# First MLP: ten inner tiles of the second half by seven block products, and the state space set-up within the first half

## The reference

```python
def _sq_relu_mlp(h, w_up, w_down):
    u = jax.nn.relu(h @ w_up)          # w_up: 1024 x 4096
    return (u * u) @ w_down            # w_down: 4096 x 1024

for i in range(DEPTH):                 # DEPTH = 2
    hn = _rmsnorm(h, norm_attn[i])
    h = h + _even_mixer(...) if i % 2 == 0 else h + _odd_mixer(...)
    h = h + _sq_relu_mlp(_rmsnorm(h, norm_mlp[i]), w_up[i], w_down[i])
```

## Time and profile before

| | |
|---|---|
| time, median of 3 runs | 2095.04 us (2094.91 to 2095.3) |
| profiled execution: its time | 2094.85 us |
| profiled execution: its span | 2092.7 us |
| instructions in the span | 35077 |
| busy share: TensorE matmul, weight load, VectorE, ScalarE, GpSimd | 99%, 87%, 65%, 42%, 40% |

### The profile page before, as it was taken

The page is one execution under the profiler, slowest core; times in us unless marked ns, Lnnn a source line. Parts: engine busy times, 40 slices in busy tenths (PEclk is TensorE's granted clock), DMA queues, the critical chain, the costliest instruction groups (busy, mean ns, idle before and its releaser), DMA issues.

```text
span 2092.7 us, 35077 instructions
## 1 busy us (share of the span) xinstructions
PE 2079.1 (99%) x14278; PEld 1826.3 (87%) x14278; DVE 1355.1 (65%) x2083; ACT 879.5 (42%) x1454; POOL 829.0 (40%) x388
## 2 busy tenths in 40 slices
PE   9999999999999999999999999999999999999998
PEld 9998899999999777798898788888888788988897
DVE  6678766625723395675855769576774577666865
ACT  5368644223323493443434423344433433433344
POOL 3343434434444453423234443333434443344332
PEclk9999999999999999999999999999999999999999
DMA  6620245233433602323343465233333332433341
GB/s 180 168 59 2 57 136 150 88 117 105 136 91 102 180 2 81 101 87 106 85 117 97 131 136 159 71 84 89 88 91 91 91 94 79 122 91 100 89 122 61
DMA packets 375695, 211.18 MB, mean 101 GB/s; under 512 B 26915, under 2 KB 368132, under 8 KB 374648
## 3 DMA queue, kind: packets, MB, share of 16 engines
q1 hardware_dynamic: 365230, 192.62, 32.6%
q10 hardware_dynamic: 10314, 16.41, 2.8%
HBM read 196.97 MB, written 15.40 MB: 101 GB/s over the span
## 4 chain that ended last, share of the span: by engine, by line
PE 65%; issue 22%; POOL 10%; DVE 2%; ACT 0%; DMA 0%; POOLq 0%; SPq 0%; DVEq 0%; ACTq 0%
PE acc L1268 15%; PE acc L1269 15%; PE acc L1270 14%; POOL w_lo L1038 9%; PE acc L1358 2%; PE ops L1427 2%; PE acc L1679 1%; PE acc L1671 1%; PE acc L1669 1%; PE tps L1367 1%; PE acc L1141 1%; PE ops L1421 1%; PE acc L1142 1%; PE acc L1143 1%; PE tps L1679 1%
## 5 line engine op out<-in xcount | busy, mean ns | idle before, releaser
L1038 POOL TENSOR_TENSOR w_lo<-raw,w_hi 128x1024 fp32r<-128x1024 f32 x278 | 688.2, 2476 | 964.8 <-ACT w_hi L1999 954.3
L1999 ACT ACTIVATE w_hi<-raw 128x1024 fp32r<-128x1024 f32 x277 | 293.4, 1059 | 839.9 <-PE acc L1270 810.5
L1268 PE MATMUL acc<-hr_hi,w_hi 128*128 128x512 f32 x1056 | 421.5, 399 | 0.3 <-POOL w_lo L1038 0.3
L1270 PE MATMUL acc<-hr_hi,w_lo 128*128 128x512 f32 x1056 | 417.7, 396 | 0.0
L1269 PE MATMUL acc<-hr_lo,w_hi 128*128 128x512 f32 x1056 | 417.6, 395 | 0.0
L1268 PE MATMUL acc<-hn_hi,w_hi 128*128 128x264 f32 (+1 forms) x840 | 246.8, 294 | 0.4 <-POOL w_lo L1038 0.4
L1270 PE MATMUL acc<-hn_hi,w_lo 128*128 128x264 f32 (+1 forms) x840 | 244.2, 291 | 0.0
L1269 PE MATMUL acc<-hn_lo,w_hi 128*128 128x264 f32 (+1 forms) x840 | 244.2, 291 | 0.0
L1268 PEld LDWEIGHTS acc<-hr_hi,w_hi 128*128 128x128 f32 x1056 | 198.5, 188 | 48.6 <-issue 1.5
L1270 PEld LDWEIGHTS acc<-hr_hi,w_lo 128*128 128x128 f32 x1056 | 198.4, 188 | 47.9
L1269 PEld LDWEIGHTS acc<-hr_lo,w_hi 128*128 128x128 f32 x1056 | 198.5, 188 | 47.1 <-issue 0.7
(11 more groups left out here) (551 smaller groups left out, 4389.0 us busy)
## 6 DMA issues: line engine op xcount, KB each, us to landing
raw<-in_w_up SPq DMA_DIRECT2D x64, 512.0 KB, 4.4
raw<-in_w_in SPq DMA_DIRECT2D x56, 512.0 KB, 3.8
raw<-in_w_down SPq DMA_DIRECT2D x40, 512.0 KB, 3.6
blocks<-in_w_down SPq DMA_DIRECT2D x32, 384.0 KB, 3.4
raw<-in_w_ffn_gate SPq DMA_DIRECT2D x22, 512.0 KB, 3.9
raw<-in_w_ffn_up SPq DMA_DIRECT2D x22, 512.0 KB, 3.8
raw<-in_w_in_even SPq DMA_DIRECT2D x18, 512.0 KB, 6.9
blocks<-in_w_ffn_down SPq DMA_DIRECT2D x16, 384.0 KB, 3.5
```

The source lines that it names most:

```text
L1038: nc.gpsimd.tensor_tensor(w_lo[:, part], raw[:, slot], w_hi[:, part].bitcast(F32), ALU.subtract).then_inc(sems["lo"], T.up("lo"))
L1268: mm(out, w_hi[:, part, w0 + k, :], xh, start=s0, stop=False)
L1270: ins = mm(out, w_lo[:, part, w0 + k, :], xh, start=False, stop=s1)
L1999: fn(w_hi[:, n % 2], raw[:, n % 4], ACT.Copy).then_inc(sems["hi"], T.up("hi"))
```

## The change

The second half of the first MLP is split. Its first ten inner tiles (`first_part`) are made in pairs and their down projection is done by the 7 block products, with token halves of 264 columns; the six that are left (`left_up`, `left_down`) are done plainly, with one unit of 6 tiles for each output tile. The forms, sums and blocks get buffers of their own, some of which lie over the buffers of the set-up, so the set-up must be over before them: VectorE does two steps in tiles 11, 12 and 13 of `up00`, `kernel_products` stands after tile 1 of `down00` instead of tile 4, the turns of the tables follow after tiles 2 to 5, and tiles 5, 6 and 7 of `down00` take 4, 5 and 6 steps. `store_ca` stands at tile 1 of `first_part`. SyncE waits for the stored tables and for the first pair's sums before it loads the blocks. The helpers of the products take the part's number and pick buffers and widths by it. GpSimd's list is cut at the same places.

```diff
-PART_SIZES = (PART_TILES, PART_TILES, 10, PART_TILES)
+FIRST_TILES = 10
+PART_SIZES = (FIRST_TILES, PART_TILES, PART_TILES, 10, PART_TILES)
...
+    first_part = Projection("first_part", [[(w_up[0], MLP_HALF * P, 0, 8, "hn")]], FIRST_TILES, 2, peel=FIRST_TILES // 2)
+    left_up = Projection("left_up", [[(w_up[0], LEFT_AT * P, 0, 8, "hn")]], LEFT_TILES, 2, peel=LEFT_TILES // 2)
+    left_down = Projection("left_down", [[(w_down[0], 0, LEFT_AT, LEFT_TILES, "mid")]], DT, 4, peel=2)
...
-    for half in range(2):
-        order += [mlp_up(0, half), mlp_down(0, half)]
+    order += [mlp_up(0, 0), mlp_down(0, 0), first_part, left_up, left_down]
...
+            first_hi = sb(s, "first_hi", [P, 7, FIRST_TILES // 2, HALF], F32R)
+            first_lo = sb(s, "first_lo", [P, 7, FIRST_TILES // 2, HALF], F32R)
...
+            pair_first = sb(s, "pair_first", [P, 2, LEN])
+            sums_first = sb(s, "sums_first", [P, 4, HALF])
+            blocks_first = sb(s, "blocks_first", [P, 6, FIRST_TILES // 2, P])
...
+        def first_bank(q, ring):
+            b = q.g % 2 if q.part else (ring + q.g) % 2
+            return acc[b][:, 1, halves_of(q.part)[0]]
...
+            units(first_part)
+            for name in ("ends_out0", "ends_out1"):
+                T.saw(name, 4 * 16)
+                sp.wait_ge(sems[name], T.at(name))
+            sp.wait_ge(sems["ssm_out"], 4 * 16)
+            sp.wait_ge(sems["pair_sums"], 1)
+            part_blocks(0)
+            units(left_up)
+            units(left_down)
...
-                tables = {4: kernel_products, 5: lambda: (turn_powers(0), turn_kernel()),
-                          6: lambda: turn_powers(1), 7: lambda: turn_powers(2)}
...
-                project(by_name["up01"], None, None, None, {0: lambda: turn_powers(3)})
-                project(by_name["down01"], None, ("hidden_lo", MLP_HALF))
...
+                tables = {1: kernel_products, 2: lambda: (turn_powers(0), turn_kernel()),
+                          3: lambda: turn_powers(1), 4: lambda: turn_powers(2), 5: lambda: turn_powers(3)}
...
+                project(first_part)
+                down_by_products(0)
+                pe.wait_ge(sems["product_kept"], QUADS[2].done(P7))
+                project(left_up, None, None, lambda: pe.wait_ge(sems["product_kept"], QUADS[3].done(P7)))
+                project(left_down, None, ("hidden_lo", LEFT_TILES))
...
-                if m == 13:
+                if m == 1:
                     T.saw("ssm_tab", 3)
...
+                def hidden(m, s, t, b):
+                    inner(m, s, b)
+                    for _ in range(2 if m in (11, 12, 13) else 1):
+                        next(setup)
+                    inner_low(m, s)
+
+                def plain(m, s, t, b):
+                    dve.wait_ge(sems[f"full{b}"], T.at(f"full{b}"))
+                    store(v.tensor_tensor(h[:, m, :], h[:, m, :], acc1[b], ALU.add), b)
+                    for _ in range({5: 4, 6: 5, 7: 6}.get(m, 1)):
+                        next(setup)
...
+                project(by_name["up00"], hidden)
+                project(by_name["down00"], plain)
+                assert not list(setup)
...
+                inner_part(0, first_part, pair_first, acc1, rstd[:])
+                project(left_up, hidden_left)
+                residual(left_down, 8, False)
```

More of the change, by code:

```diff
@@ L346, in transposed_blocks_program @@
     N_UNITS = sum(x.count for x in order)
-    BEHIND = [sum(x.count for x in order[:order.index(pj) + 1]) for pj in up_parts + [ffn_in, ffn_rest]]
+    BEHIND = [sum(x.count for x in order[:order.index(pj) + 1]) for pj in [first_part] + up_parts + [ffn_in, ffn_rest]]
     loads = [len(u) - 4 for x in order for _ in range(x.steps) for t in x.step for u in t]
@@ L977, in part_blocks @@
                         load_blocks(q)
-            for part, pj in enumerate(up_parts):
+            units(by_name["up00"], {**{2 + n: lambda n=n: spread_bands(n) for n in range(8)},
+                                    **{10 + x: lambda x=x: spread_lead(x) for x in range(2)}})
+            units(by_name["down00"])
+            units(first_part)
[7 more added lines that the diff above has]
+            units(left_down)
+            units(odd_kv)
+            units(odd_q, {2 + n: lambda n=n: bias_c_load(n) for n in range(4)})
+            units(odd_last)
+            units(odd_out)
+            for part, pj in enumerate(up_parts, 1):
                 units(pj)
@@ L1631, in down_by_products @@
                 pairs = PART_SIZES[part] // 2
+                forms_hi, forms_lo = forms_of(part)
+                columns, ring = halves_of(part)[0], T.ring[""]
                 def ready(i, k):
@@ L2372, in _ @@
             residual(even_out, 16, False)
[L2374 to L2389, removed]
             def product_high(q, i):
@@ new lines, in mlp, with hidden_slot, hidden @@
+            def mlp(parameters, tables, store_ca):
+                def hidden_slot(m, s, t, b):
+                    x = hid[:, s % 2, :]
+                    stored(b)
+                    fn(x, x, ACT.Square).then_inc(sems["hidden_full"], T.up("hidden_full"))
+                    act.wait_ge(sems["hidden_full"], T.at("hidden_full"))
+                    fn(tile(mid_hi, m), x, ACT.Copy).then_inc(sems["hidden_hi"], T.up("hidden_hi"))
+                def hidden(m, s, t, b):
+                    hidden_slot(m, s, t, b)
+                    parameters(m)
+                project(by_name["up00"], hidden, first=first_stats, carry=True)
+                project(by_name["down00"], lambda m, s, t, b: tables(m))
+                inner_part(0, first_part, pair_first, more=store_ca)
+                project(left_up, hidden_slot, carry=True)
+                residual(left_down, 8, False)
@@ L3311, in ssm_setup @@
                     sems[f"o_stored{o}"], T.up(f"o_stored{o}"))
-                for _ in range(5):
+                for _ in range(4):
                     yield
```

242 lines of the change are left out of this document (126 added, 116 removed).

## The result

The changed kernel takes 2098.72 us (median of 20 runs, 2096.29 to 2100.01); the kernel before takes 2095.19 us in its 20 runs beside it (2094.43 to 2096.0). The ratio is 1.0015 with an interval of 1.0009 to 1.0021: some 3.5 us slower. The interval leaves out 1, so the change does make the kernel slower; at the 0.2% that the prediction set as its bound it reads as no change, though the upper end of the interval stands just above it. The forecast was 2095.8 us. The execution that was profiled took 2097.7 us, with a span of 2095.9 us.

What follows compares the result with a forecast made beforehand. TensorE, busy 99%, was taken to pace the kernel by its number of matmuls. -6.8 + 3.55 + 2.1 + 0.9 + 0.75 + 0.3 = +0.8 us gave 2095.8 us; range of this case 2092.1 to 2099, with rivals 2090.6 to 2100.8.

Steps and rivals of the forecast that it cites:

- The matmuls: Second half's down projection: 420 matmuls by products at 51.1 us replace 480 plain ones at 57.9, a gain of 6.8 us.
- mid_lo of tile 15: down00's first tile: TensorE waits for VectorE's late low part, ready at 391.7, wanted at 388.15; loss 3.55 us, up to 5.1.
- a hold of less than 2.3 us: Sign of being wrong: GpSimd holding VectorE for less than 2.3 us per unit of weights.
- Rival 1: Both chains of moved VectorE steps end in time, leaving only the smaller waits: -4.9 us, 2090.2 us; chance 14%.
- The bank of first_part's third tile: TensorE waits for a bank behind VectorE's six steps after down00's tile 7; loss 2.1 us.
- The upper end, 3.0: Upper loss for the bank wait at first_part's third tile, if a VectorE step runs into a third hold: 3.0 us.
- Start of the products: Change from first_part to its products: P5 waits for the last sums_low, 0.9 us.
- left_down: Its sixth inner tile is wanted before left_up's last low part is ready: a wait of 0.75 us.
- Reopening: After the products TensorE waits for GpSimd's low part of the next weights, 0.3 us.
- What was priced at nothing: VectorE in a quad (12.5 us at 12.8), left_down's chain (0.5 us to spare), SyncE's block loads (cover 8 us): no wait.
- rival 3: Late queues delay the first blocks beyond tile 6, or left_down's chain exceeds its tile: 4 us more, 2099.8 us; chance 8%.
- Rival 2, the clock: TensorE's clock falls in the new waits, 2.5 us lost a fall: one 2098.3 us, both 2100.8; chance 18%.

Runs made afterwards that it cites:

- e5: Changed kernel with tile 15's low part before its set-up, power steps in down00's pauses, double steps in up00 tiles 11, 12, 15: 2089.51 us, ratio 0.9972.
- e6: Kernel before with only the set-up moved, spread as in e5, no products in the first MLP: 2094.88 us, ratio 1.0.
- e1: Changed kernel with the low part of up00's tile 15 written ahead of that tile's set-up step: 2094.47 us, ratio 0.9999.
- e3: Changed kernel with the edits of e1 and e2 together: 2091.01 us, ratio 0.9983.
- e2: Changed kernel with the three power steps in pauses of down00's tiles 2 to 4, so tile 7 does three steps: 2094.27 us, ratio 0.9996.
- e7: Changed kernel run again with no edit, for a second profile and more times: 2098.78 us, ratio 1.0017.
- e4: Kernel before with only the set-up moved as in the change, no products in the first MLP: 2102.45 us, ratio 1.0036.
- e8: Changed kernel with 3, 4 and 8 steps in down00's tiles 5, 6, 7, for a longer bank wait: 2101.41 us, ratio 1.0028.

## Why the prediction was right, and where its sum was short

**The matmuls (-6.8).** From 541.53 to 593.65 are 52.12 us; less the wait of 0.71 and the gap of 0.27 the 420 of the products take 51.14 us, 0.1218 each, where 51.1 was forecast, and 480 plain ones at 0.1207 are 57.9: -6.8. Shown, by the products alone too: with their own waits the prediction has -6.8 + 0.9 + 0.75 + 0.3 = -4.85, and e5 against e6 gives -4.95 in the trace.

**mid_lo of tile 15 (+3.55).** 0.78 us for the bank of tile 14 and 2.84 for mid_lo, 3.6. The forecast put the low part at 391.7; it came at 392.27, with TensorE itself 0.45 later in this trace. The list of VectorE's work with a hold for each unit was right: from the evacuation of tile 10 to that low part are 43.3 us, and 43.2 were forecast, with seven operations of GpSimd in them. The price of a hold was read a little high. The rows give 2.1 to 2.2 us (4.54 less twice 1.22 before; 3.44 less 1.23, and 2.64 less 0.42, after), not 2.25 to 2.3; it hardly shows, as the same figure was taken off the steps' lengths first. The prediction had named a hold of less than 2.3 us as a sign that it is wrong: the sign came, and the chain was priced right all the same. Rival 1, that the chains end in time, falls with it: e1 to e3 remove the waits and gain what they cost.

**The bank of first_part's third tile (+2.1).** This is the term that was mis-sized: 3.05 us. The evacuation that TensorE wants ends 14.3 us after tile 7's begins, not 13.5. Counting the chain on VectorE, the tile's evacuation takes 0.6, the three large steps 5.8 with their hold as forecast, the power steps 6.9 where 4.0 + 2.3 were counted, then 0.23 us passes before the evacuation starts. The second and third power steps were priced by the steps of tiles 12 and 13 at 1.15 and 1.3 us and take 1.34 and 1.52. The upper end, 3.0, was put down to a third hold; the value came, the hold did not, so that it fits is luck.

**The small waits.** Start of the products: 0.71 against 0.9. left_down: 0.73 against 0.75. Reopening: 0.27 against 0.3, though no trace names GpSimd's low part as what ended it. What was priced at nothing (a quad on VectorE, left_down's chain, SyncE's queue) shows no wait in any trace of ten tiles, so rival 3 falls; the end of the products is shown to be near its limit only with eight tiles.

**The sum** of the measured terms is -6.8 + 3.6 + 3.05 + 0.7 + 0.7 + 0.3 = +1.6 us for +0.8 forecast; the first MLP grew by 1.95. Most of the rest is a cost that the sum had at nothing: the first matmul after each of these waits starts 0.20 to 0.23 us ahead of the next instead of 0.12 (495.02 and 495.25), 0.1 us a wait. On the median of before, 2095.19, the 1.95 make 2097.1 us.

**Rival 2, the clock.** The remaining 1.6 us, of a miss of 2.9, are put down to it. It was priced as an alternative at full cost, 2.5 us a fall, and stood in the sum at nothing. The price was read from slow matmuls at the kernel's start, and wrongly: there the profile of the kernel before gives a granted clock of 1.00, so nothing shows that they ran at half speed.

```profile
0.00:5.00 5.00, 3.89 (x18) 3.89 (x19) 0.27 (x4) 0.00 (x0) 0.19 (x4) 1.00 0.59 166
```

What the runs showed is a mixture: a fall costs 1.3 to 1.7 us, it comes behind some of these waits and not behind others, and so it lifts the median by a part and widens the spread. With two such waits in the changed kernel, four falls in nine waits and some 1.4 us a fall, an estimate from these traces is 1.25 us; that the clock makes up all of the 1.6 us is not shown. The prediction held by a narrow margin and with luck: the median lies 0.3 us under the upper end of the range, seven of the 20 times lie above that end, and the end was added up from longer waits, not from the clock. That the medians of e1, e2 and e3 fall by 2.0, 0.8 and 2.2 us more than their waits, that the times of e7 go with the clock and that e2 has two bunches point to the same cause; the traces of e1, e4, e7 and e8 show the falls themselves. The Trainium skill ("TensorE: Matmul & The Clock Gate", What's actually happening) calls the low clock the default, which activity lifts; the prediction read from it that a wait with work close on both sides need not cost anything, and these traces show that one of 2.6 us in the list (2.8 by the starts of the matmuls) can.

## What to carry to other kernels

A gain counted in instructions of the bounding engine came out to 0.1 us here; what ate it was work of another engine moved to make room, and that could be spread so that it cost nothing. Before work is moved into tiles that have little slack, list the engine's work tile by tile, holds included, and put what TensorE waits for ahead of what it does not. A wait of TensorE of the size of these costs its length and, in part of the executions, a fall of its clock on top; so look at the spread of the times as well as at one trace: one profiled execution may be one in which it did not happen.

## What the runs showed of the hardware

- Of nine waits of TensorE of 2.6 to 2.9 us with dense matmuls before and after, four were followed by 264-column matmuls every 0.22 us instead of 0.12, at a granted clock of 0.50, for some 3.4 us that began between 0.6 us before the end of the wait and 1.1 after it; the same wait of the same kernel (mid_lo, the changed kernel and e7) did it in one execution and not in another. Behind the wait of 5.2 us the low clock lasted 6.8 us. The cost was 1.3 to 1.7 us each time, the longer one too, since half of that stretch was still the wait.
- The hold of VectorE by GpSimd was no shorter for a small operation of VectorE: two of 16 columns took 2.64 us for 0.42. It also goes the other way: where VectorE's pair had begun 0.45 us earlier (481.26), GpSimd's operation at 481.71 took 3.03 us, for 2.39 at 487.51.
- A 264-column matmul in dense work took 0.1207 us in plain stages and 0.1218 in the products (51.14 us for 420).
